# Score products with the queries' high and low rows in one operand of 128 rows

## The reference

```python
u = rmsnorm(x, mix_norm[l]) @ w_in[l]
y_conv = conformer_conv(u[..., :c0], conv_w[l], conv_b[l], conv_ln_g[l], conv_ln_b[l])
y_attn = windowed_gqa_sink(u[..., c0:c1], u[..., c1:c2], u[..., c2:], attn_sink[l])
...
kb = jnp.concatenate([kp[:, 0:nb], kp[:, 1:nb + 1], kp[:, 2:nb + 2]], axis=2)
scores = jnp.einsum("bnqkgd,bnskd->bnkgqs", q, kb).astype(jnp.float32) * scale
scores = jnp.where(valid[None, :, None, None], scores + bias[None, None], -jnp.inf)
m = jnp.maximum(jnp.max(scores, axis=-1, keepdims=True), sink_b)
p = jnp.exp(scores - m)
denom = jnp.sum(p, axis=-1, keepdims=True) + jnp.exp(sink_b - m)
o = jnp.einsum("bnkgqs,bnskd->bnqkgd", (p / denom).astype(v.dtype), vb)
```

## Time and profile before

| | |
|---|---|
| three runs, median | 1803.83 us (1803.7 to 1803.89) |
| profiled execution, its own time | 1803.68 us |
| its span | 1801.9 us, so 1.8 us lie around the span |
| PE busy | 1785.1 us, 99% |
| DVE, ACT, POOL busy | 874.6, 760.2, 1040.1 us |
| granted clock of PE | full in all 40 slices |

### The profile page before, as it was taken

The page is one execution under the profiler, slowest core; times in us unless marked ns, Lnnn a source line. Parts: engine busy times, 40 slices in busy tenths (PEclk is TensorE's granted clock), DMA queues, the critical chain, the costliest instruction groups (busy, mean ns, idle before and its releaser), DMA issues.

```text
span 1801.9 us, 23613 instructions
## 1 busy us (share of the span) xinstructions
PE 1785.1 (99%) x8186; PEld 1470.1 (82%) x8186; DVE 874.6 (49%) x1142; ACT 760.2 (42%) x1009; POOL 1040.1 (58%) x514
## 2 busy tenths in 40 slices
PE   9999999999999999999999999999999999999998
PEld 7888888888688888888888888888886888888886
DVE  7444442279866444432254444322997664444112
ACT  6333332257864333322243333222677543333222
POOL 5444457769475444457744444577793754444674
PEclk9999999999999999999999999999999999999999
DMA  5223223331123222223332232333211232232332
GB/s 199 93 94 103 89 76 98 111 101 65 48 71 106 93 93 99 84 82 97 117 106 93 95 102 81 83 98 118 84 53 49 93 105 93 93 102 76 88 97 70
DMA packets 53417, 166.66 MB, mean 92 GB/s; under 512 B 6000, under 2 KB 6256, under 8 KB 53360
## 3 DMA queue, kind: packets, MB, share of 16 engines
q1 hardware_dynamic: 52128, 163.78, 29.0%
q10 hardware_dynamic: 1232, 2.10, 0.3%
HBM read 163.76 MB, written 2.10 MB: 92 GB/s over the span
## 4 chain that ended last, share of the span: by engine, by line
PE 98%; DVE 1%; issue 0%; ACT 0%; DMA 0%; POOL 0%; POOLq 0%; ACTq 0%; DVEq 0%
PE bank L1296 31%; PE bank L1297 31%; PE bank L1298 31%; PE bank L1499 1%; PE bank L1487 1%; PE bank L1475 1%; PE bank L1477 0%; PE bank L1476 0%; PE bank L1335 0%; PE bank L1512 0%; DMA x<-xT 0%; PE bank L1326 0%; PE bank L1383 0%; DVE xs_lo L885 0%; PE bank L1380 0%
## 5 line engine op out<-in xcount | busy, mean ns | idle before, releaser
L437 POOL TENSOR_TENSOR w_lo<-stage,w_hi 128x1024 fp32r<-128x1024 f32 x351 | 863.0, 2460 | 703.0 <-ACT w_hi L565 693.6
L565 ACT ACTIVATE w_hi<-stage 128x1024 fp32r<-128x1024 f32 x351 | 371.6, 1060 | 880.9 <-PE bank L1298 880.4
L1296 PE MATMUL bank<-xs_hi,w_hi 128*128 128x512 f32 (+1 forms) x1696 | 657.4, 388 | 0.0
L1298 PE MATMUL bank<-xs_hi,w_lo 128*128 128x512 f32 (+1 forms) x1696 | 656.5, 387 | 0.0
L1297 PE MATMUL bank<-xs_lo,w_hi 128*128 128x512 f32 (+1 forms) x1696 | 656.4, 387 | 0.0
L1296 PEld LDWEIGHTS bank<-xs_hi,w_hi 128*128 128x128 f32 x1696 | 318.5, 188 | 66.3 <-issue 1.6
L1298 PEld LDWEIGHTS bank<-xs_hi,w_lo 128*128 128x128 f32 x1696 | 318.5, 188 | 64.9
L1297 PEld LDWEIGHTS bank<-xs_lo,w_hi 128*128 128x128 f32 x1696 | 318.6, 188 | 64.0
L917 DVE TENSOR_TENSOR work<-bank,rstd 128x512 f32<-128x512 f32 x176 | 120.5, 690 | 405.5 <-PE bank L1298 404.9
L1296 PE MATMUL bank<-h_hi,w_hi 128*128 128x512 f32 x704 | 273.9, 389 | 0.0
L1297 PE MATMUL bank<-h_lo,w_hi 128*128 128x512 f32 x704 | 273.9, 389 | 0.0
(11 more groups left out here) (173 smaller groups left out, 1185.3 us busy)
## 6 DMA issues: line engine op xcount, KB each, us to landing
stage<-w_gu SPq DMA_DIRECT2D x176, 512.0 KB, 3.3
stage<-w_down SPq DMA_DIRECT2D x64, 384.0 KB, 3.1
stage<-w_down SPq DMA_DIRECT2D x64, 320.0 KB, 2.9
stage<-w_in SPq DMA_DIRECT2D x24, 512.0 KB, 3.3
stage<-w_out SPq DMA_DIRECT2D x16, 512.0 KB, 3.3
x<-xT ACTq DMA_DIRECT2D x4, 512.0 KB, 6.8
stage<-w_in SPq DMA_DIRECT2D x8, 256.0 KB, 2.7
out<-result SPq DMA_DIRECT2D x8, 256.0 KB, 2.3
```

The lines of the kernel that those rows point to most:

```text
L437: nc.gpsimd.tensor_tensor(w_lo[:, r, :], stage[:, r, :], w_hi[:, r, :].bitcast(F32), ALU.subtract).then_inc(split, 1)
L565: nc.scalar.activation(w_hi[:, r, :], stage[:, r, :], ACT.Copy).then_inc(hi_made, 1)
L1296: nc.tensor.matmul(to, wh, mh, start=first, stop=False)
L1298: return nc.tensor.matmul(to, wl, mh, start=False, stop=last)
```

## The change

The queries' tile keeps, for each key head kv, one operand of 128 rows `q_pair[:, kv]`: rows of key head kv hold the high part, the other 64 rows the low part of the same head. `k_hi` and `k_lo` hold the same part twice, in both halves. Then `q_pair` by `k_hi` is high by high plus low by high, and `q_pair` by `k_lo` is high by low (plus low by low, which was left out before). Two products stand in place of three. The zeroing of `k_hi` and `k_lo` goes. ACT makes each high part of the queries in two instructions of 64 rows and copies the keys' parts to the other half in four (`double_high_k` after tile 8, `double_low_k` after tile 9); DVE makes each low part in two instructions of 64 rows. Four taps of DVE move from the tiles q0 to q3 into the attention stretch.

```diff
-V_SPREAD = [0, 3, 5, 6, 6, 7, 5, 6, 5, 5, 5, 5, 3, 1]
+V_SPREAD = [0, 3, 5, 6, 6, 7, 5, 6, 5, 4, 4, 4, 2, 1]
-LATE_TAPS = [0, 0] + [0, 1] * 5 + [1] * 8 + [3]
+LATE_TAPS = [0, 1] * 6 + [1] * 8 + [6]
...
-            q_hi = sb("q_hi", [P, NC, SEQ], F32R, region)
-            q_lo = sb("q_lo", [P, NC, SEQ], F32R, region)
+            q_pair = sb("q_pair", [P, N_KV_HEADS, NC, SEQ], F32R, region)
...
-        y_hi, y_lo = q_hi, q_lo
+        y_hi, y_lo = q_pair[:, 0], q_pair[:, 1]
...
+        def half(kv):
+            return slice(HEAD_DIM * kv, HEAD_DIM * (kv + 1))
...
-                def high_qk(t, hi):
+                def high_q(t, c):
                     scaled_ready(t)
-                    nc.scalar.activation(hi, in_bank(t)[:], ACT.Copy).then_inc(qk_hi, 1)
+                    for kv in range(N_KV_HEADS):
+                        nc.scalar.activation(q_pair[half(kv), kv, c, :], in_bank(t)[half(kv), :],
+                                             ACT.Copy).then_inc(qk_hi, 1)
+
+                def double_high_k():
+
+                    for kv in range(N_KV_HEADS):
+                        act.wait_ge(qk_hi, l * N_KV_HEADS * (NC + 1) + kv + 1)
+                        nc.scalar.activation(k_hi[half(1 - kv), kv, :], k_hi[half(kv), kv, :].bitcast(F32),
+                                             ACT.Copy).then_inc(k_doubled, 1)
+
+                def double_low_k(t):
+
+                    act.wait_ge(k_low, l + 1)
+                    tile_ready(t)
+                    for kv in range(N_KV_HEADS):
+                        nc.scalar.activation(k_lo[half(1 - kv), kv, :], k_lo[half(kv), kv, :].bitcast(F32),
+                                             ACT.Copy).then_inc(k_doubled, 1)
...
                     products(done, P_SPREAD[t])
                     done += P_SPREAD[t]
-                high_qk(12, q_hi[:, 3, :])
+                    if name == "k":
+                        double_high_k()
+                    elif name == "q0":
+                        double_low_k(IN_TILES.index("k"))
+                high_q(12, 3)
...
                 def low_q(t, c):
-                    hi, lo = q_hi[:, c, :], q_lo[:, c, :]
-                    dve.wait_ge(qk_hi, l * (NC + 2) + c + 3)
-                    nc.vector.tensor_tensor(lo, in_bank(t)[:], hi.bitcast(F32), ALU.subtract).then_inc(evicted, 1)
+                    for kv in range(N_KV_HEADS):
+                        dve.wait_ge(qk_hi, l * N_KV_HEADS * (NC + 1) + N_KV_HEADS * (c + 1) + kv + 1)
+                        low = nc.vector.tensor_tensor(q_pair[half(1 - kv), kv, c, :], in_bank(t)[half(kv), :],
+                                                      q_pair[half(kv), kv, c, :].bitcast(F32), ALU.subtract)
+                    low.then_inc(evicted, 1)
...
-                for kv in range(N_KV_HEADS):
-                    other = slice(HEAD_DIM * (1 - kv), HEAD_DIM * (2 - kv))
-                    nc.vector.memset(k_hi[other, kv, :].bitcast(F32), 0.0).then_inc(k_padded, 1)
-                    nc.vector.memset(k_lo[other, kv, :].bitcast(F32), 0.0).then_inc(k_padded, 1)
...
-                    nc.tensor.matmul(to, q_hi[:, c, q], k_hi[:, kv, keys], start=True, stop=False)
-                    nc.tensor.matmul(to, q_hi[:, c, q], k_lo[:, kv, keys], start=False, stop=False)
-                    nc.tensor.matmul(to, q_lo[:, c, q], k_hi[:, kv, keys], start=False,
+                    nc.tensor.matmul(to, q_pair[:, kv, c, q], k_hi[:, kv, keys], start=True, stop=False)
+                    nc.tensor.matmul(to, q_pair[:, kv, c, q], k_lo[:, kv, keys], start=False,
                                      stop=True).then_inc(scored, 1)
...
-                pe.wait_ge(k_padded, l * 5 + 5)
+                pe.wait_ge(k_doubled, (l + 1) * 2 * N_KV_HEADS)
```

More of the change, by code:

```diff
@@ L301, in encoder @@
         pt_made = sem("pt_made")
-        k_padded = sem("k_padded")
+        k_low = sem("k_low")
+        k_doubled = sem("k_doubled")
         scores_taken = sem("scores_taken")
@@ L676, in high_k @@
                     for kv in range(N_KV_HEADS):
-                        rows = slice(HEAD_DIM * kv, HEAD_DIM * (kv + 1))
-                        nc.scalar.activation(k_hi[rows, kv, :], in_bank(t)[rows, :], ACT.Copy).then_inc(qk_hi, 1)
+                        nc.scalar.activation(k_hi[half(kv), kv, :], in_bank(t)[half(kv), :],
+                                             ACT.Copy).then_inc(qk_hi, 1)
                 def exp_scores(g, c):
@@ L740, in _ @@
                     elif name[0] == "q":
-                        high_qk(t, q_hi[:, int(name[1]), :])
+                        high_q(t, int(name[1]))
                     if t in FIRST_TAP_AT:
@@ L1038, in low_k @@
                     for kv in range(N_KV_HEADS):
[L1039 to L1042, removed]
+                        dve.wait_ge(qk_hi, l * N_KV_HEADS * (NC + 1) + kv + 1)
+                        nc.vector.tensor_tensor(k_lo[half(kv), kv, :], in_bank(t)[half(kv), :],
+                                                k_hi[half(kv), kv, :].bitcast(F32),
+                                                ALU.subtract).then_inc(*((evicted, 1) if kv else (k_low, 1)))
                 def low_q(t, c):
-                    hi, lo = q_hi[:, c, :], q_lo[:, c, :]
-                    dve.wait_ge(qk_hi, l * (NC + 2) + c + 3)
-                    nc.vector.tensor_tensor(lo, in_bank(t)[:], hi.bitcast(F32), ALU.subtract).then_inc(evicted, 1)
+                    for kv in range(N_KV_HEADS):
[3 more added lines that the diff above has]
+                    low.then_inc(evicted, 1)
                 def taps(first, count):
```

## The result

| | before | after |
|---|---|---|
| median | 1803.7 us (1803.56 to 1803.89, 5 runs) | 1812.81 us (1811.01 to 1813.99, 5 runs) |
| ratio after to before | | 1.005, 95% interval 1.0035 to 1.0064 |
| profiled execution, its span | 1803.68, 1801.9 us | 1812.96, 1811.1 us |
| PE, DVE, ACT busy | 1785.1, 874.6, 760.2 us | 1782.9, 879.5, 772.1 us |
| chain of waits | PE 98%, DVE 1% | PE 93%, DVE 3%, ACT 2%, issue 2% |

What follows compares the result with a forecast made beforehand. PE bounds the kernel by the chain of waits, but ACT and DVE pace the attention stretch. Terms 0 + 0 + 0.65 us a layer, +1.3 us for both, bring 1803.68 to 1805.0 us; range 1800.6 to 1807.2.

Steps and rivals of the forecast that it cites:

- What bounds the kernel: Whole kernel: PE is full in the tiles, ACT sets its pace to 464 us; fewer products bring at most 9.4 us.
- The middle terms: First attention units to 464 us and units 11 to 19: 0 each, ends -0.5 to +0.5 and -0.7 to +0.7 us.
- the first of them: Units to 464 us: 0, as ACT paces PE without gaps and one more DVE tap cancels closing ACT's earlier idle.
- rival C: Attention stretch: DVE is the bound and each of four moved taps lands, about 5.8 us slower, 1809.5 us; chance 0.07.
- C's own sign: Unit 11's scores: DVE reaches them later than PE gives them, so the 1.17 us gap is gone.
- Input tiles, "+0.1": Input tiles: slack covers ACT's 4.8 us a layer of extra instructions; only the last tile ends 0.1 us later.
- Block 1's division, "0.65": Units 19 to 25: three more taps delay block 1's division and PE loses 0.5 to 0.9 us a layer, taken as 0.65.
- the upper ends: Per layer, the largest values of the terms, added as 0.65 + 0.5 + 0.7, 3.7 us in all, giving 1807.2.
- the third term: Units 19 to 25, at block 1's division: PE loses 0.65 us a layer, between 0.5 and 0.9.
- Rival D: Input tiles: ACT's copies are not covered and scores or weights wait, up to 4.8 us a layer, 1813.3 us; chance 0.02.

Runs made afterwards that it cites:

- e1: The kernel before without its second score product (high queries by low keys), nothing else touched: 1800.95 us, ratio 0.9985.
- e6: The changed kernel with 9 products of zeros in each layer where PE waits for block 1's division: 1809.49 us, ratio 1.0033.
- e9: The changed kernel with queries' high halves ahead of ACT's weight rounding and DVE's taps and merge put where DVE had waited: 1801.57 us, ratio 0.9989.
- e8: The changed kernel with queries' high halves first, no extra tap early in the units, five taps ahead of block 1's division, two behind: 1803.42 us.
- e7: The changed kernel with the last sum over channels reading a PSUM bank in place of `y_conv` in SBUF: 1806.83 us, ratio 1.0018.
- e3: The changed kernel with both tap tables of the kernel before, so the four taps are back in the query tiles: 1807.22 us, ratio 1.0021.

## Why the prediction was wrong

**What bounds the kernel: right.** PE's 9.4 us of products were mostly not to be had; e1 shows 2.6 of them. The middle terms (0 for the units to 464 us, 0 for units 11 to 19) hold within their ends: the lateness goes from 0.82 us at the first bias (DVE) to 0.62 behind block 0's division (PE). The reason given for the first of them held only in part. ACT is not busy all through 455 to 464 us (8.62 of 9.00), and DVE is (8.92): rival C's mechanism in part, with PE waiting for DVE's maxima up to 0.7 us at a time. C's own sign, DVE's waits for score products gone, did not show: 0.68 us of the 1.17 are left. They should have stayed near 4 us in all, though, and are 2.6 (2.3 and 0.3 in the view of waits): DVE came late out of the tiles and made up part of it there.

**Input tiles, "+0.1": the step that failed was what the slack was asked to cover.** The text found ACT's slack ahead of the rounding, and asked only whether POOL and PE would see a late rounding. They did not (PE 25.00 of 25.00 and POOL 24.53 as before). But DVE's low halves stand behind that same rounding, and it was DVE that waited, three times. What was queued behind the late instruction on ACT's own queue was not followed; only the last tile was. Measured: 0.82 us at the first bias, 0.62 us at PE.

**Block 1's division, "0.65": the mechanism was right, the size was not.** That this was the place, that the division turns from waiting on ACT to being late, and that nothing behind has slack, all held. The term came to 2.3 us. The three taps cost 2.38 us, a little over the upper end of 2.3. The rest is two things the term left out: DVE came to the taps 0.56 us late in place of 0.1 early (the tiles), and the sum took 2.03 us in place of 0.69. The sum's duration was taken over from a row in which POOL did nothing; moved by some 3 us, it met POOL's weight parts. Their row stands in the profile of before (timeline of POOL):

```profile
480.07 4.68 POOL L437 TENSOR_TENSOR w_lo<-stage,w_hi 128x1024 fp32r<-128x1024 f32 x2
```

Had the sum's new start, about 480.5 us by the prediction's own numbers, been laid beside this row, the overlap was there to be read.

**The clock: missing from the sum.** No step asked what a wait of more than two microseconds does to PE behind it. It was worth 1.5 us a layer, a third of the loss (e6), and it hung on the two terms above: with the wait at 0.91 or 1.03 us there is none.

Together 0.62 + 2.34 + 1.53 = 4.49 us a layer, where 0.65 was forecast. The range could not cover this, and its upper end was also added up short: with the third term's own end of 0.9 us, the upper ends are 4.2 us and not 3.7, so 1807.9 and not 1807.2.

**Rival D** had the nearest number (1813.3) by another way: ACT's copies were not covered, but PE never stood idle from 418 to 443 us (its scores waited 0.8 us for `q_pair` behind that), and what was lost up to block 0's division was 0.6 us a layer, not 4.8. That its number came near is luck: the rest of the loss was at the division and in the clock, which D did not name.

## What to carry to other kernels

When work is moved later, carry each moved or shifted instruction's new start to the rows of every other engine, since its old duration holds only beside its old neighbours; and of an instruction that gets later, follow everything queued behind it on its own engine, not only who reads its result. Where an engine other than PE sets the pace, a saving on PE pays only as far as that engine has gaps, so move its spare work into the gaps (e9), not to the end. A wait on PE should be priced with the products behind it as well: fill it or keep it short.

## What the runs showed of the hardware

- PE's granted clock fell behind a wait of 2.38 us, in both layers: 0.69 in the mean over 5.5 us, and the same products took 5.30 us in place of 3.77. It did not behind waits of 1.44 us (e8), 1.03 us (e7) and 0.91 us, nor behind 1.71 us in the profiled run of e3, while seven other runs of e3 showed a lower mean clock, at a place that no trace shows. With zero products of 2.17 us in the wait of 2.38 the same products took 3.77 us again (e6).
- A DVE sum of two SBUF operands took 0.69 us alone and 1.79, 2.03 and 2.58 us beside POOL's weight parts, which themselves took 5.12 in place of 4.67 us in one of the three cases. With one operand in PSUM it took 0.69 us beside the same POOL work.
- ACT's and DVE's instructions on 64 rows cost as much as on 128 (0.60 and 0.70 us for 512 columns, from PSUM); ACT's copy of 64 rows from SBUF to SBUF took 0.64. So splitting by key head doubled their time.
- A score product took as much of PE with 128 live rows in it as with 64 rows of zeros: 0.12 us for 256 columns and 0.17 for 384.
